# A fused two-block layer on one core: eight modulation products and a projection piece moved in the first block, and the handovers of the mixer output made whole

## The reference

```
mod = silu(c) @ w_ada + b_ada                       # 1024 x 6144
h = rmsnorm(x) * (1 + scale_m) + shift_m
rq, rk, rv, rg, aq, ak, av = split(h @ w_in)        # 1024 x 3072
y_ret = silu(rg) * bidirectional_retention(rq, rk, rv)
y_att = sum of dilated attentions (8 heads of 64) of aq, ak, av
mixed = concat([y_ret, y_att]) @ w_out              # 1024 x 1024
x = x + gate_m * rmsnorm(mixed)
h = rmsnorm(x) * (1 + scale_f) + shift_f            # then router, 16 experts
```

## Time and profile before

| what | value |
|---|---|
| median of 3 runs | 2400.32 us (2396.76 to 2400.93) |
| profiled execution, its own time | 2400.93 us |
| its span | 2398.9 us |
| TensorE busy | 1921.8 us (80%) |
| VectorE busy | 969.2 us (40%) |
| ScalarE busy | 696.0 us (29%) |
| mean granted TensorE clock | 0.895 |

### The profile page before, as it was taken

One profiled execution on the slowest core, in us unless ns is written; L12 is line 12 of the kernel. 1 busy time (PEld: TensorE's weight loads), 2 busy tenths in 40 slices (PEclk: granted clock), 3 DMA queues, 4 the chain that ended last, 5 costly groups with the idle time before them and its releaser, 6 DMA issues.

```text
span 2398.9 us, 34233 instructions
## 1 busy us (share of the span) xinstructions
PE 1921.8 (80%) x12667; PEld 1366.8 (57%) x12667; DVE 969.2 (40%) x1348; ACT 696.0 (29%) x963; POOL 40.6 (2%) x68
## 2 busy tenths in 40 slices
PE   6996655655555555565899999899989999989998
PEld 4774111211111111111799877799879988778997
DVE  3474000000000000000676576666656666666665
ACT  4331000000000000000444455444444444544443
POOL 0000000000000000000000000000000000000000
PEclk9997778778787778778999999999999999999999
DMA  9767999999999999999556553355535565344561
GB/s 370 251 241 331 429 428 429 428 428 429 428 428 428 428 428 428 428 428 410 181 199 217 163 157 123 122 176 196 189 107 182 186 203 176 124 136 150 171 208 55
DMA packets 174825, 660.85 MB, mean 275 GB/s; under 512 B 10053, under 2 KB 108142, under 8 KB 143734
## 3 DMA queue, kind: packets, MB, share of 16 engines
q1 hardware_dynamic: 171980, 654.12, 70.4%
q10 hardware_dynamic: 2376, 3.03, 0.6%
q0 software_dynamic: 352, 2.11, 0.2%
HBM read 656.60 MB, written 2.64 MB: 275 GB/s over the span
## 4 chain that ended last, share of the span: by engine, by line
issue 77%; PE 17%; DVE 3%; ACT 1%; POOL 1%; DMA 1%; POOLq 0%; ACTq 0%; DVEq 0%; PEldq 0%; PEld 0%
PE PS L1862 12%; PE PS L1577 2%; DVE units L205 1%; DVE arena L205 1%; DMA ring<-in_w_ada 1%; PE PS L1546 1%; ACT units L205 0%; POOL arena L604 0%; PE PS L1643 0%; PE PS L1661 0%; DVE hn L205 0%; POOLq L603 0%; POOLq L629 0%; DVE x L205 0%; DVE hT_split L205 0%
## 5 line engine op out<-in xcount | busy, mean ns | idle before, releaser
L205 DVE TENSOR_TENSOR units<-ring,units 128x1024 fp32r<-128x1024 f32 (+2 forms) x416 | 505.7, 1216 | 206.7 <-ACT units L205 172.1
L205 ACT ACTIVATE units<-ring 128x1024 fp32r<-128x1024 f32 (+2 forms) x416 | 438.0, 1053 | 482.7 <-PE PS L1862 447.4
L1862 PE MATMUL PS<-hT_split,units 128*128 128x256 f32 x4416 | 554.9, 286 | 10.0 <-DVE hT_split L205 8.4
L1862 PEld LDWEIGHTS PS<-hT_split,units 128*128 128x128 f32 x4416 | 547.8, 194 | 20.5 <-DVE hT_split L205 11.3
L205 DVE SCALAR_TENSOR_TENSOR arena<-arena,PS 128x512 f32<-128x512 f32 (+1 forms) x54 | 41.4, 767 | 802.5 <-ACT arena L205 513.1
L205 ACT ACTIVATE arena<-PS 32x256 f32<-32x256 f32 (+4 forms) x135 | 66.8, 495 | 945.9 <-PE PS L1832 310.7
L1862 PE MATMUL PS<-units,hT_split 128*128 128x512 f32 (+2 forms) x1248 | 294.2, 396 | 13.3 <-DVE hT_split L205 9.0
L1862 PEld LDWEIGHTS PS<-units,hT_split 128*128 128x128 f32 x1248 | 238.1, 195 | 61.3 <-DVE hT_split L205 9.8
L1862 PE MATMUL PS<-units,hid_split 128*128 128x512 f32 x1056 | 255.6, 392 | 0.0
L1862 PEld LDWEIGHTS PS<-units,hid_split 128*128 128x128 f32 x1056 | 192.8, 189 | 37.0 <-issue 0.9
L1824 PE MATMUL PS<-moe_ring,arena 128*32 128x512 f32 x768 | 124.5, 781 | 98.9 <-DMA moe_ring<-in_w_gate_e 55.8
(11 more groups left out here) (208 smaller groups left out, 1254.7 us busy)
## 6 DMA issues: line engine op xcount, KB each, us to landing
ring<-in_ffn_wi SPq DMA_DIRECT2D x88, 1024.0 KB, 5.4
ring<-in_w_gate_e SPq DMA_DIRECT2D x24, 2048.0 KB, 36.0
moe_ring<-in_w_up_e SPq DMA_DIRECT2D x24, 2048.0 KB, 36.4
ring<-in_w_down_e SPq DMA_DIRECT2D x24, 2048.0 KB, 35.6
moe_ring<-in_w_gate_e SPq DMA_DIRECT2D x24, 2048.0 KB, 36.7
ring<-in_w_up_e SPq DMA_DIRECT2D x24, 2048.0 KB, 36.5
moe_ring<-in_w_down_e SPq DMA_DIRECT2D x24, 2048.0 KB, 36.2
ring<-in_ffn_wo SPq DMA_DIRECT2D x44, 1024.0 KB, 4.9
```

The source lines that it names most:

```text
L205: return instruction(*args, **kwargs)
L1862: passes = [mm(out, lhs[i], rhs[j], start=start and i + j == 0, stop=stop and i == 1, **flags) for i, j in ((0, 0), (0, 1), (1, 0))]
```

## The change

TensorE's order: rqk's first half moves from before head 0 to behind its first turn, rqk's second half from head 0 to head 1, and the `w_ada` products 8 to 11 follow them in pairs. Products 20 to 23 move from between the first y transposes and the first `out_rows` to head 5. The y transposes of each half are signalled once instead of twice, the attention half goes to banks 6 and 7, and `out_rows` runs for both token tiles on the attention half before retention's half is transposed. SyncE's order follows (`ADA_AFTER`): rqk's second half becomes position 17 instead of 15, `w_ada` slots 8 and 9 become 15 and 16, and slots 20 to 23 come ahead of rg. ScalarE and VectorE get their own orders to match: unit 14 is split ahead of head 0 and unit 15 between heads 0 and 1; the gated retention of tile 0 is computed ahead of attention's output; `ada_row(2)` moves ahead.

```diff
 IN_PIECES = [("ak", 2048), ("aq", 1536), ("av", 2560), ("rqk", 0), ("rv", 512), ("rg", 1024)]
-ADA_AFTER = {("rqk", 1): 4, ("rv", 0): 2, ("rv", 1): 6, ("rg", 1): 4}
+ADA_AFTER = {("rqk", 0): 2, ("rqk", 1): 2, ("rv", 0): 2, ("rv", 1): 10}
 POS_IN, POS_ADA, _pos = {}, list(range(KT)), KT
...
                                     mod_rows[i].partition_broadcast(P)).then_inc(S["mod_full"], 16)
-                if i == 0:
-                    inverse_root("var_ret", 1, head_ms[:, :], eps_group, "head_roots")
+            inverse_root("var_ret", 1, head_ms[:, :], eps_group, "head_roots")
             for t in range(NT):
...
                 S["skew_written"], 16)
-            first_hi(*range(8, 14))
+            first_hi(*range(8, 15))
...
             att_exp(0)
+            first_hi(15)
             att_exp(1)
...
                     att_exp(h + 2)
+                if h < 2:
+                    first_hi(16 + 2 * h, 17 + 2 * h)
+                if h == 5:
+                    first_hi(20, 21, 22, 23)
                 if h == 1:
...
                     activation(qkT.rearrange("p a n -> p (a n)"), two_banks(0), ACT.Copy).then_inc(S["cols_copied"], 1)
-                if h < 3:
-                    first_hi(14 + 2 * h, 15 + 2 * h)
-                if h == 5:
-                    first_hi(20, 21, 22, 23)
                 if h == 6:
...
             first_hi(24, 25, 26)
+            act.wait_ge(S["first_T"], 3)
+            y_hi(6, 4)
+            y_hi(7, 6)
+            first_hi(27)
             gate_tanh(1)
-            for turn, (bank, k) in enumerate(((0, 4), (1, 6), (4, 0), (5, 2))):
-                act.wait_ge(S["first_T"], 3 + turn)
-                y_hi(bank, k)
-                if turn == 1:
-                    first_hi(27)
             first_hi(28, 29, 30, 31)
+            act.wait_ge(S["first_T"], 4)
+            y_hi(4, 0)
+            y_hi(5, 2)
...
             for t in range(NT):
-                act.wait_ge(S["first_T"], t + 7)
+                act.wait_ge(S["first_T"], t + 5)
                 activation(hT[:, 0:4, t * P:(t + 1) * P], PS[:, 4 + 2 * t, :].rearrange("p (k n) -> p k n", k=4),
...
                 if done == 2:
-                    first_lo(*range(10, 14))
+                    first_lo(*range(10, 15))
...
             att_scores(0)
+            first_lo(15)
             att_scores(1)
...
                 att_scores(h)
-                if h < 5:
-                    first_lo(10 + 2 * h, 11 + 2 * h)
+                if h < 4:
+                    first_lo(12 + 2 * h, 13 + 2 * h)
             dve.wait_ge(S["late_full"], 112)
...
             ret_weight(3)
-            first_lo(20, 21, 22, 23)
+            first_lo(20, 21)
+            ada_row(2, b_late[:, 1, :])
+            first_lo(22, 23)
...
             dve.run(V.reduce_sum, by_head(head_ms[:, :]), heads(hn[:, :, HALF:D], RET_H), AX.X).then_inc(S["var_ret"], 1)
+            dve.wait_ge(S["head_roots"], 1)
+            tt(yc, yc, wide_of(by_head(head_ms[:, :]), RET_DV), ALU.mult)
+
+            def gated_y(t):
+                dve.wait_ge(S["rg_tanh"], t + 1)
+                stt(rg[:, t, :], rg_tanh[:, t, :], 1.0, PS[:, 4 + t, :], ALU.add, ALU.mult)
+                stt(hn[:, t, 0:HALF], hn[:, t, 0:HALF], 0.5, rg[:, t, :], ALU.mult, ALU.mult).then_inc(S["y_rows"], 1)
+
+            gated_y(0)
             dve.wait_ge(S["att_p"], ATT_H)
...
                wide_of(att_stat[:, 2, :, :].rearrange("p h t -> p t h"), DH), ALU.mult).then_inc(S["y_rows"], 1)
-            first_lo(24, 25)
-            dve.wait_ge(S["head_roots"], 1)
-            tt(yc, yc, wide_of(by_head(head_ms[:, :]), RET_DV), ALU.mult)
-
-            def gated_y(t):
-                dve.wait_ge(S["rg_tanh"], t + 1)
-                stt(rg[:, t, :], rg_tanh[:, t, :], 1.0, PS[:, 4 + t, :], ALU.add, ALU.mult)
-                stt(hn[:, t, 0:HALF], hn[:, t, 0:HALF], 0.5, rg[:, t, :], ALU.mult, ALU.mult).then_inc(S["y_rows"], 1)
...
-            y_lo(1, 0, 4)
-            y_lo(2, 1, 6)
-            first_lo(26)
-            gated_y(0)
+            first_lo(24, 25, 26)
+            y_lo(1, 6, 4)
+            y_lo(2, 7, 6)
             first_lo(27)
             gated_y(1)
-            ada_row(2, b_late[:, 1, :])
+            first_lo(28, 29, 30, 31)
             y_lo(3, 4, 0)
             y_lo(4, 5, 2)
-            first_lo(28, 29, 30, 31)
...
             for t in range(NT):
-                dve.wait_ge(S["first_T"], t + 7)
+                dve.wait_ge(S["first_T"], t + 5)
                 dve.run(V.tensor_copy, hT[:, 4:8, t * P:(t + 1) * P],
...
             att_s(1)
-            in_columns("rqk", 0, 0)
             pe.wait_ge(S["in_copied"], 2)
...
                 if h == 0:
+                    in_columns("rqk", 0, 0)
+                    ada_products(8, 2)
+                elif h == 1:
                     in_columns("rqk", 0, 1)
                     piece_end()
-                elif h == 1:
-                    ada_products(8, 4)
+                    ada_products(10, 2)
                 elif h == 2:
...
                         ret_s(g)
+                    ada_products(20, 4)
                 elif h == 6:
...
-            def y_turns(first, bank):
-
-                for k in range(first, first + 4):
-                    for t in range(NT):
-                        last = y_turn(k, t, bank)
-                    if k % 2 == 1:
-                        last.then_inc(S["first_T"], 1)
+            pe.wait_ge(S["att_pT"], ATT_H)
+            pe.wait_ge(S["y_rows"], 2)
+            for k in range(4, KT):
+                for t in range(NT):
+                    last = y_turn(k, t, 6)
+            last.then_inc(S["first_T"], 1)
+            pe.wait_ge(S["gn_read"], 1)
+            pe.wait_ge(S["first_hT"], KT + 2)
...
-            pe.wait_ge(S["gn_read"], 1)
-            pe.wait_ge(S["y_rows"], 1)
-            y_turns(4, 0)
-            ada_products(20, 4)
-            pe.wait_ge(S["first_hT"], KT + 2)
-            out_rows(0, range(4, KT))
+            for t in range(NT):
+                out_rows(t, range(4, KT))
             pe.wait_ge(S["y_rows"], 3)
-            y_turns(0, 4)
-            out_rows(1, range(4, KT))
+            for k in range(4):
+                for t in range(NT):
+                    last = y_turn(k, t, 4)
+            last.then_inc(S["first_T"], 1)
             pe.wait_ge(S["first_hT"], KT + 4)
...
             out_rows(1, range(4))

```

More of the change, by code:

```diff
@@ L1110, in _ @@
             dve.run(V.reduce_sum, by_head(head_ms[:, :]), heads(hn[:, :, HALF:D], RET_H), AX.X).then_inc(S["var_ret"], 1)
-            dve.wait_ge(S["att_p"], ATT_H)
-            dve.run(V.reciprocal, att_stat[:, 2, :, :], att_stat[:, 1, :, :])
-            dve.wait_ge(S["att_av"], ATT_H)
-            tt(heads(hn[:, :, HALF:D], ATT_H), heads(PS[:, 2:4, :], ATT_H),
-               wide_of(att_stat[:, 2, :, :].rearrange("p h t -> p t h"), DH), ALU.mult).then_inc(S["y_rows"], 1)
-            first_lo(24, 25)
             dve.wait_ge(S["head_roots"], 1)
@@ L1123, in gated_y @@
                 stt(hn[:, t, 0:HALF], hn[:, t, 0:HALF], 0.5, rg[:, t, :], ALU.mult, ALU.mult).then_inc(S["y_rows"], 1)
+            gated_y(0)
+            dve.wait_ge(S["att_p"], ATT_H)
+            dve.run(V.reciprocal, att_stat[:, 2, :, :], att_stat[:, 1, :, :])
+            dve.wait_ge(S["att_av"], ATT_H)
+            tt(heads(hn[:, :, HALF:D], ATT_H), heads(PS[:, 2:4, :], ATT_H),
+               wide_of(att_stat[:, 2, :, :].rearrange("p h t -> p t h"), DH), ALU.mult).then_inc(S["y_rows"], 1)
             def y_lo(turn, bank, k):
```

## The result

| | before | after |
|---|---|---|
| median of 4 runs each | 2400.62 us (2396.76 to 2402.32) | 2429.92 us (2425.84 to 2435.50) |
| ratio, with its 95% interval | 1 | 1.0127 [1.0107, 1.0146] |
| profiled execution, its own time | 2400.93 us | 2427.81 us |
| span | 2398.9 us | 2425.8 us |
| end of `w_out`'s products | 181.13 us | 213.75 us |

The change costs 29.3 us, 1.3%. The prediction was 2419 (2407 to 2432), so its direction and range hold. Its likeliest case (2412 to 2427) is missed by 3 us: the measured time lies near the top of the range, where the late landing (2429 to 2437) stood, and two of the four runs (2433.68 and 2435.50) lie beyond it.

What follows compares the result with a forecast made beforehand. The prediction took the experts' stage as bound by its weight transfer and TensorE as the bound before it; delays of 16.4 us plus 1.9 of slow clock made +18.3 on 2400.93, so 2419 us (2407 to 2432).

Steps and rivals of the forecast that it cites:

- likeliest case: The transfer of rqk's second half lands between 74 and 86 us; kernel time 2412 to 2427, chance 0.64.
- late landing: That transfer lands only when `skew` is through, 88 to 97 us; kernel time 2429 to 2437, chance 0.13.
- rv's products start later: On TensorE, rv's products start at 111.7 instead of 105.17, behind the delayed head 0: +6.5 us.
- hole ahead of the first y transposes: TensorE waits for attention's output, which VectorE makes after the wait for GpSimd's roots: +1.0 us.
- hole behind them: TensorE waits after the first y transposes while VectorE splits units 24 to 26 ahead of both `y_lo`: +4.3 us.
- slow clock in the first two `out_rows`: Slower TensorE clock charged to the 4.3 us hole only, nothing for the 3.1 us one: +1.9 us.
- second handover: After retention's half is transposed, TensorE waits for roundings and rests queued behind the last splits: +3.1 us.
- landing of position 17: rqk's second half, issued at 60.05 beside the `skew` write, lands at 78.5 us; bounds 65.3 and 96.6.
- roots' move: GpSimd's roots behind both `mod_rows` steps cost nothing: second step over near 153, statistics arriving near 159.
- Early landing: The transfer of rqk's second half lands before 71.4 us: +7.6, kernel time 2408, chance 0.12.
- Nothing: Waits of 1 to 4 us shrink as VectorE runs ahead, and the transfer lands early: 2398 to 2405, chance 0.07.
- Faster: The 7.24 us hole at rqk's second half goes and nothing its size replaces it: 2393.7, chance 0.04.

Runs made afterwards that it cites:

- skew_late: The changed kernel with ScalarE's write of `skew` issued only after head 1's exponentials; median 2441.56 us, ratio 1.0183.
- rqk_pos15: The changed kernel with rqk's second half back at position 15, ahead of `w_ada` slots 8 to 11; median 2423.47 us, ratio 1.0102.
- front_only: The kernel before with only the earlier half of the change (rqk, products 8 to 11, splits of units 14 to 19); median 2414.73 us, ratio 1.0070.
- roots_first: The changed kernel with GpSimd's roots back between the two `mod_rows` steps; median 2431.68 us, ratio 1.0131.
- lo_order: The changed kernel with VectorE's two `y_lo` steps ahead of its splits of units 25 and 26; 2430.30 us, one run.
- tail_only: The kernel before with only the later half of the change (products 20 to 23 in head 5, y handovers, roots); median 2415.77 us, ratio 1.0067.
- pos15_copy_first: The changed kernel with rqk's second half at position 15 and ScalarE's copy of rqk ahead of rv's splits; median 2420.48 us, ratio 1.0095.
- early_split: The kernel before with only units 14 and 15 of rqk split ahead of head 0 on both engines; median 2391.84 us, ratio 0.9974.
- second_cover: tail_only with retention's half transposed ahead of the second `out_rows`, and `y_hi` and `y_lo` ahead of units 28 to 31; median 2411.20 us, ratio 1.0053.
- tail_fixed: second_cover plus the edits of roots_first and lo_order; median 2408.40 us, ratio 1.0038.

## Why the prediction was right, and what it sized wrong

Direction and mechanism were right, and the range held in part by luck. At the first expert product the change costs 32.8 us, which on the median before would have been 2433, beyond the range's end of 2432; the 3.5 us that brought the median back are counted as scatter below.

The prediction walked to the end of `w_out` in steps. Its sum was +18.3; the changed kernel has 213.75 - 181.13 = +32.6:

| step | predicted | measured |
|---|---|---|
| rv's products start later | +6.5 | +13.2 |
| slow clock in rv's first half (7.35 against 5.73) | 0 | +1.6 |
| wait for a `w_ada` slot in head 5 | +1.7 | +0.6 |
| other gaps up to the last rg product | 0 | +0.8 |
| hole ahead of the first y transposes | +1.0 | +6.4 |
| these transposes at slow clock (1.94 against 1.0) | 0 | +0.9 |
| hole behind them | +4.3 | +3.5 |
| slow clock in the first two `out_rows` (13.96 against 11.06) | +1.9 | +2.9 |
| second handover | +3.1 | +3.1 |
| small gaps that go | -0.2 | -0.4 |

**The landing of position 17 was mis-sized.** The mechanism is the predicted one: the slot travels beside `skew` (skew_late), head 0 waits behind the split that needs it, and 12.3 of the 15.95 go when the slot is early (rqk_pos15). But I took 78.5, from two rows of which one was a slot of the other kind, and it was 84.2. That is 5.7 of the 6.7 that rv's start is off. The other 1.0 is the clock: head 0's turn and scores took 3.0 instead of the 1.5 I gave them, since the lower level already holds when the hole ends, and not only in the piece behind it; the shorter wait ahead of rv (1.04 against 1.3) and a first half of 7.65 instead of 7.95 give a little back.

Beside the `skew` write, position 17 took 22.3 to 24.2 us as a `w_in` slot (four kernels: the changed one, front_only, roots_first, lo_order) and 13.6 to 19.1 as a `w_ada` slot (seven kernels: the kernel before, rqk_pos15, tail_only, pos15_copy_first, early_split, second_cover, tail_fixed). The rule that the prediction cites from the Trainium skill ("DMA: Bandwidth & Descriptors", Queues, rings and completion order), that engines take turns between queues a whole packet at a time, agrees in direction with these rows: the transfer in 2 KB pieces is the slower one. The prediction tied four times the turns to its upper bound, 36.5 us after the issue, without working it out; no row reaches it. Piece size wasn't tested by itself, as the two kinds also meet different neighbours.

**The roots' move was priced at nothing, and costs 3.2.** The prediction had the second `mod_rows` step over near 153, six ahead of the statistics. In the trace its read was issued only at 166.40 and landed 6.2 later, at 172.6, while the statistics came at 169.1: the step was not over. The pause between the two steps of the roots, 0.33 before, took 3.50 (roots_first has 0.33 again). Seven kernels have the read ahead of the roots, and their traces tell what ends the pause:

| kernel | read issued | landed | second step of the roots | after the landing |
|---|---|---|---|---|
| after | 166.40 | 172.6 | 172.89 | 0.3 |
| rqk_pos15 | 160.45 | 166.35 | 166.65 | 0.3 |
| skew_late | 172.33 | 178.0 | 178.34 | 0.3 |
| tail_only | 150.87 | 157.5 | 157.74 | 0.3 |
| pos15_copy_first | 151.64 | 158.2 | 158.59 | 0.35 |
| lo_order | 162.29 | 169.3 | 169.62 | 0.3 |
| second_cover | 150.85 | 157.75 | 158.04 | 0.3 |

The pause takes 3.07 to 3.50, and the read 5.7 to 7.0 from its issue, yet the second step starts 0.3 after the landing each time. So the second step was held until GpSimd's own read had landed, although no semaphore in the program asks for that.

**The first handover starts later than its sum.** 1.0 was predicted and 6.4 measured: 3.2 are the roots. The rest, 2.2, is in VectorE's rows ahead of them. The statistics start 9.4 before the last rg product ends and not 11.6: `ada_row(2)` now stands between the two pairs of splits (0.79 with its gap), which the prediction had put at nothing too, rg's second half took 13.3 from its issue where I used 12.5, and the rest is handoffs.

One cause of this hole was left untested. In the kernel before, VectorE makes attention's output ahead of its wait for the roots, so the first y transposes don't depend on them. The change puts the gating of tile 0, and with it that wait, in front. In the changed kernel's trace the last product with the values ends at 169.96 and the last rg product at 172.77; attention's output is a reciprocal of 0.25 and a step of 1.22. By these rows it could have been ready near 171.5, ahead of TensorE, with or without the roots' 3.2. This is an estimate: no run puts attention's output back in front.

**The clock.** Around the handovers I gave the slow clock to one of three holes. The changed kernel shows it in head 0's turn and scores, in rv's first half behind a hole of 1.04, and in y's first transposes and `out_rows`: 1.5 + 1.6 + 0.9 + 2.9 = 6.9 beside the predicted cost of rqk's first half, where 1.9 stood in the sum. For the lone hole of 3.12 the value of nothing was right here (11.18), though not in tail_only (12.78).

**One for one.** Over all kernels with a median of several runs, the shift of the first expert product and that of the median agree within 4 us, from -7.4 to +39.0. The changed kernel is at one end of that: +32.8, and +29.3 in the medians. In its trace the lead of the kernel before is still 32.5 near 1340 us. In the second block it falls and rises by 1 to 1.7 at a time (30.9 at 1354, 32.5 again at 1415), and falls more than it rises. At the first of these steps the clock is 0.96 in the kernel before (1350 to 1380) and 1.00 in the same stretch after (1383 to 1413). As the stretch from the first expert product on varies by 8.8 among kernels that share its code, I count this as scatter. Why it varies stays open.

**The rivals.** Early landing: out, the slot took 23.9. Late landing: the slot came at 84.2, before the 88 at which that rival began, though the time is the one it gave (2429 to 2437). Nothing: out. Faster: out for this change, because position 17 takes the slot away; early_split, which keeps it at 15, gets it (2391.8, where 2393.7 was worked out). The 14.3 by which its sum falls short are two sizes (landing 5.7, slow clock 6.9 - 1.9 = 5.0), two costs put at nothing (roots 3.2, `ada_row(2)` 0.8) and small terms of both signs.

## What to carry to other kernels

When an item moves back in a hand-written order of slots, look up what else is on the DMA engines at its new time, and what stands behind its consumer on every engine that runs in order: here a split moved ahead of head 0 tied the whole head to one transfer. Work that stands between producing and consuming a handover is cover; before moving it, name what will lie there in its place. And the cheap trial is often to move the split alone: five lines on two engines won 7.5 us, and the reordering of all five engines lost 29.

## What the runs showed of the hardware

- A write of 1.57 MB from 8 partitions, in 1032 packets, stretches a 1 MB load in 2 KB pieces beside it from 7.7 us to between 22.3 and 24.2, in both places tried: position 17 or, when the write is later, rv's slot. A load in 8 KB pieces took 13.6 to 19.1 there.
- The pause between the two steps of the roots, where a `drain()` stands, took 3.07 to 3.50 us in seven kernels in which GpSimd had issued the read of `mod_rows` 2.6 to 3.8 us before the first of them, and 0.33 in those in which the read was issued after both. In all seven it ended 0.3 us after the read had landed. No run takes the `drain()` out, so whether it is the drain or the second step that waits stays open.
- After short holes the granted clock sometimes fell to its lower level and sometimes not. Behind the same 3.12 us, 48 matmuls of 512 columns took 11.18 in two kernels (the changed one, pos15_copy_first) and 12.8 in five (tail_only, rqk_pos15, skew_late, roots_first, lo_order). The two are those in which the 48 matmuls before had lost the most to the slow clock (13.94 and 13.96 against 12.46 to 13.53); why isn't shown. Behind 0.94 to 1.14 us ahead of rv, 24 such matmuls took 7.2 to 7.4 in four kernels (the changed one, front_only, pos15_copy_first, lo_order) and 5.76 in roots_first. In tail_fixed a hole of 2.07 was followed by 3.0 us of loss, and one of 2.24 ahead of `out_rows` by none.
